# Linear attention in halves: scores over all 128 rows, and a running state decayed by a diagonal product on TensorE

## The reference, cut to what matters

```python
def chunked_gated_linear_attention(q, k, v, log_f):
    '''S_t = diag(f_t) S_{t-1} + k_t v_t^T ; o_t = S_t^T q_t, computed chunkwise.'''
    ...
    def step(state, inp):
        qi, ki, vi, gi = inp
        cum = jnp.cumsum(gi, axis=2)
        diff = cum[:, :, :, None, :] - cum[:, :, None, :, :]
        decay = jnp.where(causal, jnp.exp(jnp.where(causal, diff, 0.0)), 0.0)
        scores = jnp.einsum('bhid,bhijd,bhjd->bhij', qi, decay, ki)
        last = cum[:, :, -1:, :]
        out = (jnp.einsum('bhij,bhjv->bhiv', scores, vi)
               + jnp.einsum('bhid,bhdv->bhiv', qi * jnp.exp(cum), state))
        state = (jnp.exp(last[:, :, 0, :, None]) * state
                 + jnp.einsum('bhjd,bhjv->bhdv', ki * jnp.exp(last - cum), vi))
        return state, out
```

## Time and profile before

| | |
|---|---|
| median of 3 runs | 3348.65 us (3347.36 to 3349.76) |
| the profiled execution | 3347.46 us, span 3345.8 us |
| busy shares of the span | PE 90%, DVE 49%, ACT 29%, POOL 21% |
| mean granted TensorE clock | 0.92 |
| `gla_stage` | from its first DVE instruction (329.67 us) to the last copy of outputs (starts at 576.21 us) |
| copies of outputs L1072 | 32, that of step 20 starts at 507.78 us |

### The profile page before, as it was taken

How to read it: one execution, slowest core, us unless ns; L and a number is a source line. 1 busy time by engine, 2 the same in 40 slices (tenths; PEclk the granted TensorE clock), 3 DMA queues, 4 the chain that set the end, 5 groups by cost and what they waited for, 6 DMA issues and landing times. The chain is left out here.

```text
span 3345.8 us, 39719 instructions
## 1 busy us (share of the span) xinstructions
PE 3018.4 (90%) x15196; PEld 2401.4 (72%) x15196; DVE 1653.0 (49%) x2819; ACT 982.9 (29%) x1921; POOL 688.4 (21%) x442
## 2 busy tenths in 40 slices
PE   6999788788999999978999799988899997999888
PEld 4767788336888888866758688866777676887766
DVE  4170773213413413332488763476524787634865
ACT  3241220111000000020267442075102674421751
POOL 1233000002333333313112301402141113014021
PEclk8999555798999999989999899999999998999989
DMA  3111000201111021113112101203231120012032
GB/s 106 35 32 35 1 1 23 82 6 63 38 57 51 32 64 51 32 69 105 27 38 70 32 1 42 79 8 126 89 106 27 39 75 26 1 51 70 7 126 89
DMA packets 78801, 168.41 MB, mean 50 GB/s; under 512 B 14848, under 2 KB 33808, under 8 KB 78096
## 3 DMA queue, kind: packets, MB, share of 16 engines
q1 hardware_dynamic: 70160, 140.61, 12.6%
q10 hardware_dynamic: 8448, 25.18, 2.7%
HBM read 128.00 MB, written 20.97 MB: 45 GB/s over the span
## 5 line engine op out<-in xcount | busy, mean ns | idle before, releaser
L296 PE MATMUL psum<-H,ffn_W 128*128 128x512 f32 x672 | 262.8, 391 | 12.8 <-POOL ffn_W L1328 11.1
L297 PE MATMUL psum<-H,ffn_W 128*128 128x512 f32 x672 | 262.4, 390 | 0.0
L298 PE MATMUL psum<-H,ffn_W 128*128 128x512 f32 x672 | 262.3, 390 | 0.0
L1326 POOL CAST ffn_W<-ffn_W 128x1024 fp32r<-128x1024 f32 (+1 forms) x84 | 69.3, 825 | 891.7 <-PE psum L298 447.5
L1623 DVE TENSOR_SCALAR_CACHE_REDUCE MB<-OM,tk_mid 128x512 bf16<-128x512 f32 (+2 forms) x192 | 184.3, 1010 | 2.3
L1592 ACT ACTIVATE MB<-OM,tk_mid 128x384 bf16<-128x384 f32 (+2 forms) x192 | 157.0, 818 | 51.8 <-DVE tk_mid L1620 48.5
L1402 DVE TENSOR_SCALAR ffn_Y<-ffn_G,ffn_par 128x1024 f32<-128x1024 f32 x21 | 22.1, 1052 | 297.6 <-ACT ffn_G L1391 297.6
L482 POOL TENSOR_TENSOR tk_W<-tk_W 128x1024 fp32r<-128x1024 f32 (+1 forms) x38 | 78.5, 2068 | 425.9 <-ACT tk_W L434 425.9
L1328 POOL TENSOR_TENSOR ffn_W<-ffn_W 128x1024 fp32r<-128x1024 f32 (+1 forms) x84 | 161.8, 1926 | 6.7
L296 PEld LDWEIGHTS psum<-H,ffn_W 128*128 128x128 f32 x672 | 126.8, 189 | 40.1 <-POOL ffn_W L1328 11.5
L298 PEld LDWEIGHTS psum<-H,ffn_W 128*128 128x128 f32 x672 | 126.7, 189 | 26.7
(11 more groups left out here) (416 smaller groups left out, 7647.4 us busy)
## 6 DMA issues: line engine op xcount, KB each, us to landing
OM<-in_w_feat SPq DMA_DIRECT2D x34, 512.0 KB, 4.4
tk_W<-in_w_feat SPq DMA_DIRECT2D x22, 512.0 KB, 3.7
ffn_W<-in_ffn_w_gate SPq DMA_DIRECT2D x21, 512.0 KB, 3.5
ffn_W<-in_ffn_w_val SPq DMA_DIRECT2D x21, 512.0 KB, 3.5
ffn_W<-in_ffn_w_down SPq DMA_DIRECT2D x42, 256.0 KB, 2.6
OM<-MB ACTq DMA_DIRECT2D x64, 128.0 KB, 2.6
OM<-OM ACTq DMA_DIRECT2D x64, 128.0 KB, 3.0
fin_W<-in_w_out SPq DMA_DIRECT2D x4, 2048.0 KB, 10.5
```

Of the source, the lines that this page charges most:

```text
L296: pe.matmul(out, a1, b1, start=start, stop=False)
L297: pe.matmul(out, a1, b2, start=False, stop=False)
L298: return pe.matmul(out, a2, b1, start=False, stop=stop)
L1326: pool.tensor_copy(w1, w).then_inc(rounded, 1)
```

## The change

- **Scores.** One matmul per level takes both heads: all 128 rows of `KW[:, n]`, and 128 columns of `QW`, which now has room for each head's queries apart, with zeros in the rows that are not the head's. VectorE multiplies the queries into `KW` in place (semaphore `lifted`); ScalarE copies each head's rows to its columns of `QW` (`part_heads`, two copies for each level; semaphore `spread`). This is done for all eight halves of the passes `v`, also for those of pass 3, where nothing else is prepared (`spread_at`). GpSimd clears the other rows (`CLEARED`, 12 memsets).
- **State.** ScalarE makes a diagonal matrix of the decay (`fade`), TensorE multiplies it with the old state and adds the update in the same bank, ScalarE copies the sum out (`carry`). VectorE's two instructions per step are gone. In the first step of a pass there is no old state: no `fade`, no diagonal product, and no product with `QE`. In the last step of a pass there is no update.
- **Exponentials.** Those of the first level and of the state's weights `KL` take the difference as a bias, per chunk: 8 instructions of 64 columns in place of 2 of 256, and 4 of 128 in place of 1 of 512. VectorE makes 2 differences fewer per half, of 8, and one small instruction more.

The diff, cut:

```diff
+    def spread_at(p, c):
+        if p == 2 and CH <= c < CH + 3:
+            return 6, c - CH
+        if p == 3 and c < 3:
+            return 7, c
+        return None
...
+    CLEARED = (0, 1, 4, 5, 6, 7)
...
-        QW = flat[:, 0:NL * HALF].rearrange("p (n c m) -> p n c m", n=NL, c=NT)
-        QK = flat[:, NL * HALF:NL * HALF + S]
+        QW = flat[:, 0:NL * S].rearrange("p (n c h m) -> p n c h m", n=NL, c=NT, h=2)
+        QK = flat[:, NL * S:]
...
+                for v in CLEARED:
+                    p, half = v // 2, v % 2
+                    if p:
+                        pool.wait_ge(out_done, NT * (p - 1) + CH * (half + 1))
+                    stale = (slice(64, P), slice(0, 64)), (), (slice(32, 64), slice(64, P)), (slice(0, 32), slice(32, 64))
+                    at = slice(CH * half, CH * (half + 1))
+                    for h, r in enumerate(stale[p]):
+                        if n:
+                            pool.wait_ge(cleared, n)
+                        pool.memset(QW[r, :, at, h, :], 0.0).then_inc(cleared, 1)
...
-                    w4 = half_of(KW[:, n, :], u).rearrange("p (c m w) -> p c m w", c=CH, w=2 * b)
-                    q4 = half_of(Q[:, g, :], u).rearrange("p (c m w) -> p c m w", c=CH, w=2 * b)
-                    own(dve.tensor_tensor(QW[:, n, CH * (u % 2):CH * (u % 2 + 1), :]
-                                          .rearrange("p c (m w) -> p c m w", w=b),
-                                          w4[:, :, :, b:2 * b], q4[:, :, :, b:2 * b], ALU.mult))
-                    w3 = half_of(KW[:, n, :], u).rearrange("p (m w) -> p m w", w=2 * b)[:, :, 0:b]
-                    k3 = half_of(K[:, g, :], u).rearrange("p (m w) -> p m w", w=2 * b)[:, :, 0:b]
-                    own(dve.tensor_tensor(w3, w3, k3, ALU.mult))
+                    w3 = half_of(KW[:, n, :], u).rearrange("p (m w) -> p m w", w=2 * b)
+                    q3 = half_of(Q[:, g, :], u).rearrange("p (m w) -> p m w", w=2 * b)
+                    k3 = half_of(K[:, g, :], u).rearrange("p (m w) -> p m w", w=2 * b)
+                    up, down = slice(b, 2 * b), slice(0, b)
+                    dve.tensor_tensor(w3[:, :, up], w3[:, :, up], q3[:, :, up], ALU.mult).then_inc(lifted, 1)
+                    own(dve.tensor_tensor(w3[:, :, down], w3[:, :, down], k3[:, :, down], ALU.mult))
...
-                            dve.wait_ge(upd_done, step + 1)
-                            for h, r in enumerate(rows):
-                                v = slice(h * 64, (h + 1) * 64)
-                                last = dve.scalar_tensor_tensor(
-                                    ST[r, (c + 1) % 2, v], ST[r, c % 2, v], EL[r, c:c + 1],
-                                    kit.psum[r, 7, v], ALU.mult, ALU.add)
-                            last.then_inc(upd_taken, 1)
-                            dve.wait_ge(upd_taken, (NT - 1) * p + c + 1)
...
-                        act.activation(half_of(KL, u), Z[:, seq % 4, :], ACT.Exp).then_inc(weights, 1)
...
+                def bend_first(u):
+
+                    act.wait_ge(cums, u + 1)
+                    c3 = half_of(C, u).rearrange("p (m w) -> p m w", w=P)
+                    w3 = half_of(KW[:, 0, :], u).rearrange("p (m w) -> p m w", w=P)
+                    for m in range(CH):
+                        c = CH * (u % 2) + m
+                        act.activation(w3[:, m, 64:P], c3[:, m, 64:P], ACT.Exp, bias=NR[:, c:c + 1])
+                        last = act.activation(w3[:, m, 0:64], c3[:, m, 0:64], ACT.Exp, scale=-1.0, bias=c3[:, m, 63:64])
+                    last.then_inc(weights, 1)
...
+                    for m in range(CH):
+                        last = act.activation(k3[:, m, :], c3[:, m, :], ACT.Exp, scale=-1.0, bias=c3[:, m, P - 1:P])
+                    last.then_inc(weights, 1)
...
+                def part_heads(v, n):
+
+                    p, half = v // 2, v % 2
+                    b = LEVELS[n]
+                    act.wait_ge(lifted, NL * min(v, 4 + half) + n + 1)
+                    act.wait_ge(cleared, 2 * len([x for x in CLEARED if x <= v]))
+                    w4 = half_of(KW[:, n, :], v).rearrange("p (c m w) -> p c m w", c=CH, w=2 * b)
+                    for h, r in enumerate(rows_in[p]):
+                        last = act.activation(QW[r, n, CH * half:CH * (half + 1), h, :]
+                                              .rearrange("p c (m w) -> p c m w", w=b), w4[r, :, :, b:2 * b], ACT.Copy)
+                    last.then_inc(spread, 1)
...
-                    for seq in ((0, 1, 2), (3, 4, TAIL), (6, 7))[part]:
-                        bend(u, seq)
+                        bend_first(u)
+                        bend(u, 1)
+                        bend(u, 2)
+                    elif part == 1:
+                        bend(u, 3)
+                        bend(u, 4)
+                        bend_state(u)
+                    else:
+                        bend(u, 5)
+                        bend(u, 6)
+                    for n in levels_of(part):
+                        part_heads(u, n)
...
+                def fade(p, c):
+
+                    n = (NT - 2) * p + c - 1
+                    if n >= 2:
+                        act.wait_ge(upd_done, (NT - 1) * ((n - 2) // (NT - 2)) + (n - 2) % (NT - 2) + 2)
+                    act.wait_ge(weights, N_Z * (2 * tile_of[p] + c // CH) + TAIL + 1)
+                    act.activation(FADE[:, n % 2, :], ident, ACT.Copy, scale=EL[:, c:c + 1]).then_inc(fading, 1)
+
+                def carry(p, c):
+                    act.wait_ge(upd_done, (NT - 1) * p + c + 1)
+                    if p >= 2 and c == 0:
+                        act.wait_ge(state_set, p - 1)
+                    if NT * p + c:
+                        act.wait_ge(out_done, NT * p + c)
+                    for h, r in enumerate(rows_in[p]):
+                        v = slice(h * 64, (h + 1) * 64)
+                        last = act.activation(ST[r, (c + 1) % 2, v], kit.psum[r, 7, v], ACT.Copy)
+                    last.then_inc(upd_taken, 1)
...
+                        if c < NT - 1:
+                            if c:
+                                fade(p, c)
+                            carry(p, c)
+                        if c % CH == CH - 1 and prep_at(p, c - 1):
+                            keys_turned(prep_at(p, c - 1)[0])
...
+                        if spread_at(p, c):
+                            v, part = spread_at(p, c)
+                            for n in levels_of(part):
+                                part_heads(v, n)
...
+                    pe.wait_ge(mixed, min(2 * p + c // CH, 5) + 1)
+                    pe.wait_ge(spread, NL * (2 * p + c // CH + 1))
                     for n in range(NL):
-                        for h, r in enumerate(rows_in[p]):
-                            pe.matmul(kit.psum[:, 2 * (step % 2) + h, n * 64:(n + 1) * 64], KW[r, n, at],
-                                      QW[r, n, c, :], start=True, stop=True)
-                    for h, r in enumerate(rows_in[p]):
-                        last = pe.matmul(kit.psum[:, 2 * (step % 2) + h, NL * 64:NL * 64 + 1], QK[r, at],
-                                         heads[r, 2 * p + h:2 * p + h + 1], start=True, stop=True)
+                        pe.matmul(bank[:, n * P:(n + 1) * P], KW[:, n, at],
+                                  QW[:, n, c, :, :].rearrange("p h m -> p (h m)"), start=True, stop=True)
+                    last = pe.matmul(bank[:, NL * P:NL * P + 2], QK[:, at], heads[:, 2 * p:2 * p + 2],
+                                     start=True, stop=True)
...
-                        pe.matmul(kit.psum[:, 7, 0:P], KLT[:, c * P:(c + 1) * P], V[:, c, v_at:v_at + P],
-                                  start=True, stop=True).then_inc(upd_done, 1)
+                        if c < NT - 1:
+                            if c:
+                                n = (NT - 2) * p + c - 1
+                                pe.wait_ge(fading, n + 1)
+                                pe.matmul(kit.psum[:, 7, 0:P], FADE[:, n % 2, :], ST[:, c % 2, :], start=True, stop=False)
+                            pe.matmul(kit.psum[:, 7, 0:P], KLT[:, c * P:(c + 1) * P], V[:, c, v_at:v_at + P],
+                                      start=c == 0, stop=True).then_inc(upd_done, 1)
...
+                        if c:
+
+                            pe.matmul(kit.psum[:, 6, 0:P], QE[:, c * P:(c + 1) * P], ST[:, c % 2, :],
+                                      start=True, stop=False)
...
```

More of the change, by code:

```diff
@@ L910, in gla_stage @@
         ST = sbuf(nc, mem, "gla_ST", [P, 2, P])
+        FADE = sbuf(nc, mem, "gla_FADE", [P, 2, P])
         LM, DM = level.bitcast(INT32), ident.bitcast(INT32)
@@ L988, in place @@
                         dve.wait_ge(out_done, step - 1)
-                    bank = kit.pair(step % 2).rearrange("p (h n) -> p h n", h=2)
+                    bank = kit.pair(step % 2)
                     first = own.n
@@ L996, in place @@
```

(22 more changed lines are left out.)

90 lines of the change are left out of this document (43 added, 47 removed).

## The result

| | before | after |
|---|---|---|
| median | 3349.2 us (4 runs) | 3381.64 us (4 runs, 3379.74 to 3382.51) |
| ratio after / before | | 1.0094, 95% interval 1.0076 to 1.0111 |
| profiled span | 3345.8 us | 3380.4 us |

The change makes the kernel 0.9% slower. Forecast were 3357.5 us and a range of 3340 to 3374: the sign was right, the time lies 7.6 us above the range.

A forecast was written before the change was run, and what follows sets the result against it. TensorE at half clock was taken to bound the stage, afterwards a chain through ScalarE's `fade` with a swinging clock. Blocks +19.1, last 11 steps -8.3 and start -2 gave +8.8: 3357.5 us, range 3340 to 3374.

The forecast's parts named there:

- the blocks: Steps 0 to 20 of `gla_stage`, five blocks of four steps with preparation: 34.6 us each, 173 before 153.9, +19.1.
- the tail: Last 11 steps of `gla_stage`: 60.1 us, before 68.4, so -8.3, taking half the clock loss.
- The chain itself: PE's step, ACT's copy, preparation part, `fade`, PE's next step, nothing beside them; loop of 0.9 us per step with `fade`.
- the clock in the blocks: TensorE's clock falls in each gap behind preparations; a cold burst runs 4.1 us at half clock, 5.3 together.
- Bound before: In `gla_stage`, some 330 to 577 us, TensorE at half clock sets the time.
- Scores: Score loads per step: 14 new take 2.9 us at half clock, 1.5 at full; merging the heads brings 0.1 us.
- ScalarE's prices: Preparation instructions on ScalarE: 0.15 us at 64 elements, 0.20 at 128, 0.32 at 256; together 10.9 us a half.
- Start: Before the stage's steps, spins wait for the state's exponentials, ready at 340.6 in place of 342.3: -2 us.
- Full clock throughout: Rival: gaps in `gla_stage` do not pull TensorE's clock down; -30.5 us, 3318 us; chance 14%.
- Clock back sooner: Rival: a cold burst in `gla_stage` is at half clock for 2 us only; -9.5 us, 3339 us; chance 16%.
- The forecast's own range: Cold bursts between 4.7 and 6.0 us and `part_heads` 20% off give 3348 to 3369 us.

The follow-up runs named there:

- e1: Changed kernel with ScalarE's `fade` of the next step directly behind the outputs' copy, ahead of the preparation part: 3320.8 us.
- e14: Changed kernel with TensorE products on constants in its gaps behind preparation parts and in the last 11 steps: 3334.5 us.
- e3: Changed kernel's scores, heads' copies and exponentials only, with VectorE's state from the kernel before: 3314.1 us.
- e7: Kernel before the change, with four TensorE products of 128 rows by 384 columns on constants ahead of step 20: 3352.4 us.

## Why the prediction was right in sign and too low

Two terms of the sum failed: the prices of ScalarE's instructions in the chain (+13 us in the blocks, +3 in the tail), and the half of the clock loss that was allowed for in the tail (+8.8). The chain itself and the clock in the blocks were right.

- **Bound before, order and chain: right.** PE idled for `fade` (88.4 us in 24 waits), the clock swung between 0.5 and 1.0, a bare step at full clock took 4.28 us, made of the 3.4 and 0.9 forecast. e1 shows the chain, e14 the clock. GpSimd's memsets (1.59 us each) were hidden.
- **Scores: right at equal clock, wrong as a verdict.** 14 loads took 1.64 or 3.11 us, as foretold, but "merging the heads brings 0.1 us" left out which clock each kind of product holds: alone it is worth 35 us (e3, e7). The sum had this for the whole change, since it priced new steps by rows of the new kind.
- **ScalarE's prices: the step that failed first.** Estimates by size alone: 0.15 at 64 and 0.20 at 128 elements, 0.32 for a head's copy. Measured: 0.24 and 0.29 apart, and 0.43 (the two or four copies of 64 rows follow each other with no overlap: 1.70 for four). A half's ScalarE work is 2.6 us more: (0.09 x 8) + (0.09 x 4) + (0.11 x 14). `fade` took 0.40 in place of 0.28, but the bare step came out at its price all the same. Without its clock loss a block whose four steps all have a `fade` took 31.1 us (e14's first, third and fifth), where 28.5 were worked out: +2.6; five times +13. The Trainium skill has the price of the operands ("ScalarE: Activation LUTs", section What ACT_TABLE_LOAD costs): about 93 ns for each per-partition pointer as scale or bias. The rows agree, 337 ns for 64 elements with one. The prediction named this danger last and didn't price it. The heads' copies have no such operand; why they don't overlap wasn't tried.
- **The clock in the blocks: right.** There are fifteen stretches at half clock, one behind each preparation part, and PE worked 4.1 us in each on average (3.3 to 5.2), as priced. Half of these 62.2 us is lost, 6.2 a block, forecast 6.1. (Against e14 a block lost 36.0 - 30.9 = 5.1, since e14 keeps two such stretches.) The prediction's "10.2 us of old steps" at full clock were 8.2: the first 2 were spins and transposes.
- **Steps counted in full.** The blocks' sum took all twenty steps as usual ones. Four are ends or starts of a pass, shorter and without a `fade`: at full clock a block with two of them takes some 28.1 us in place of 31 (35.2 less 7.1 of clock loss). Two such blocks: -6. With the +13: blocks +26.4, forecast +19.1.
- **The tail: the larger miss.** Forecast 60.1, measured 73.5. I took half the clock loss, 8.8 us (42.0 less 302 x 0.11); against e14's 55.9 it was 17.6. The copies were 12 us in place of 9. Of the 13.4, then, 8.8 are the clock, 3.0 the copies, 1.6 the rest. The gaps of 2 to 3 us that I thought half harmless pulled the clock down like the long ones, and it stayed down longer than in the blocks: in five stretches PE worked at half clock for 3.0 to 12.2 us, 37.5 in all, half of it lost. One of them, in the changed kernel:

```profile
553.10:562.00 8.90, 8.87 (x40) 8.77 (x41) 2.31 (x9) 0.71 (x3) 3.17 (x2) 0.50 0.00 0
```

- **Start:** -2 forecast, nothing measured (353.99 and 353.94); its spins wait for the same dearer exponentials and began at 342.74 in place of the forecast 340.6.
- Together 7.3 + 13.4 + 2.1 = 22.8 above the +8.8: 31.6 of the 34.6 between the two profiled executions (3382.04 and 3347.46). The other 3 lie behind the stage, where the code is the same and its time differs by up to 12 us between the traces; they can't be told from that spread.
- **Rivals.** "Full clock throughout" was put at 3318; e14, which comes near it, took 3334.5: too low by 16, of which some 5 are e14's two stretches at half clock and most of the rest ScalarE's prices. "Clock back sooner" had 2 us at half clock in a burst, measured were 4.1. The forecast's own range let the heads' copies be 20% off (they were 34% dearer); the upper end of the final range let bursts be cold but did not let the prices move.

## What to carry to other kernels

An instruction whose inputs are long known must not stand in its engine's queue behind work that waits for the latest event: moved ahead, `fade` gave back 61 and then 15 us. Judge a merge of small products by the clock that it holds, not by its issue time alone. And where a chain has nothing beside it, every term in it is the bound: price each small instruction with its operands, and let these prices move in the range.

## What was not expected of the hardware

With products of 32 rows by 64 columns the clock fell from 1.00 to 0.50 though PE was busy throughout (e7); with 128 by 128 it held 1.00 in e3's tail, PE busy 11.7 of 12.0 us. How long PE worked at 0.50 before the clock rose again differed from 3.0 to 12.2 us within the changed kernel; on what that hangs isn't shown. ScalarE's copies over 64 or 32 partitions of 256 elements start 0.43 us apart, over 128 partitions exponentials of the same length 0.31. GpSimd's copies lengthened VectorE's two-input products from 421 to 502 ns.
